# Cross attention scores from upper and lower halves in three products, with both operands split as they are read out of PSUM

## The chip, the cores and the metric

The program runs on one core of a Trainium2 chip. The metric is the device time of one execution in microseconds (us). A difference of 0.2% of this kernel's time is about what a measurement of it can tell from no change.

## The reference, cut to what matters

A block of two layers (feed forward, a mixer, cross attention to a memory of 256 tokens, feed forward) is followed by a second block with another mixer and feed forward. 512 tokens, model width 1024, all in fp32. The change is in the cross attention, which runs once in each of the two layers:

```python
def memory_cross_attention(h, m, w_q, w_kv, q_gain, k_gain, w_o):
    q = rms_norm((h @ w_q).reshape(b, s, X_HEADS, X_HEAD_DIM), q_gain)      # 4 heads of 256
    kv = (m @ w_kv).reshape(b, m.shape[1], 2, X_HEADS, X_HEAD_DIM)
    k = rms_norm(kv[:, :, 0], k_gain)
    v = kv[:, :, 1]
    sc = jnp.einsum('bqhd,bkhd->bhqk', q, k).astype(jnp.float32) * (X_HEAD_DIM ** -0.5)
    p = jax.nn.softmax(sc, axis=-1).astype(v.dtype)
    o = jnp.einsum('bhqk,bkhd->bqhd', p, v).reshape(b, s, X_HEADS * X_HEAD_DIM)
    return o @ w_o
```

## The kernel before, in words

All the large matrix products (`pe_gemm`, `pe_products`) are made from operands split into an upper and a lower half of type fp32r: the weights are brought by DMA into one of four raw buffers, ACT copies them into `wh` (the rounding to fp32r is the upper half), DVE subtracts to get `wl`, and the PE adds three products, upper by upper, upper by lower and lower by upper. Splitting runs three chunks of 256 rows ahead of the PE (`AHEAD`). What belongs to another task (an eviction, a transposition) is put beside certain chunks by the functions called `side` and behind a group by those called `evict`.

One cross attention (class `Cross`, tiles `c0...` in the first layer, `c1...` in the second) runs like this:

- `kv`: four groups of 512 columns, the values first (`c0v`, kept in fp32), then the keys. `xq`: two groups of 512 columns, the queries. For keys and queries ACT copies a 128-token tile into `c0t` and squares it, DVE sums the squares, POOL takes the power, and DVE scales the tile (`dve_head_scale`).
- `pe_turn` transposes such a group, 4 blocks of 128 columns, into four PSUM banks. `act_turned` (L884) reads out the odd blocks and `dve_turned` (L894) the even ones, both times the gain, into `c0kT` (8 blocks of 128x256) and `c0qT` (8 blocks of 128x512), fp32. For keys group 2 this is beside chunk 1 of keys group 3; for keys group 3 beside chunk 1 of queries group 0; for queries group 0 beside chunk 1 of queries group 1; and for queries group 1 it is inside the attention itself, as the function `then`.
- The attention (`pe_whole`, `act_whole`, `dve_whole`, L1295 to L1378) is a pipeline over four heads in steps `s`, below as PE sees it. "Scores" of a head are 8 products (4 tiles of 128 queries, 2 blocks of the head) of 256 columns in fp32; P is the 128x1024 tile of probabilities; "values" are 4 products of 512 columns in fp32.

```
s=0: scores 0
s=1: then (16 transpositions of queries group 1), scores 1, turn P of head 0
s=2: scores 2, turn P of head 1, values 0
s=3: scores 3, turn P of head 2, values 1
s=4: turn P of head 3, values 2        s=5: values 3
```

The order on the other two engines is fixed just so by the code. The lines that decide around the change are these: on both engines `then` comes behind the work of head 0's step 0 and ahead of what follows.

```python
    def act_whole(act, A, finish, then):
        for s in range(A.H + 3):
            if s == 1:
                then()
...
    def dve_whole(dve, A, finish, then):
        for s in range(A.H + 3):
            if s == 1:
                then()
            if 1 <= s <= A.H:
                den, rd = A.small(s - 1, 2), A.small(s - 1, 3)
                dve.wait_ge(expd, (A.tag, s - 1))
```

So ACT does the exponentials of head 0 (`cx0P<-ps,cx0sm`), then its part of the read-out of queries group 1, then the exponentials of head 1. DVE does the maxima of head 0 (`cx0sm<-ps`), then its part of the read-out, then the reciprocal and the scaling of P of head 0 (`cx0P<-cx0P,cx0sm`, L106, four instructions with the flag `normed`), then the maxima of head 1. The PE turns the four rows of a P each when its `normed` is set.

In a profile one fp32 product of the PE appears as two MATMUL records, and each product or record has its own LDWEIGHTS (PEld). Every instruction has the line of its helper: L94 is a matmul, L97 a transpose, L100 an activation, L103 a tensor_tensor, L106 a tensor_scalar, L109 a scalar_tensor_tensor, L118 a reduce, L121 a copy, L124 a reciprocal. In the list of instructions below a buffer's number stands behind its name (`cx0P_149`, `cx0P_150` are the two P tiles), and one fp32 product is one row.

Of the kernel before, what the change touches and what calls it, by code (L numbers as in the profile page):

```python
# [265 lines left out]
def program(nc, T, out):  # L266
# [1004 lines left out]
    class Whole:  # L1271
# [1 line left out]

        groups = [[0, 1], [2, 3]]

        def __init__(self, tag, H, area, scale):
            self.tag, self.H, self.scale = tag, H, scale
            self.p = [sb(f"{tag}P{i}", [P, WHOLE_W], F32, area) for i in range(2)]
            self.pt = [sb(f"{tag}PT{i}", [P, 2, S], F32, area) for i in range(2)]
            self.sm = [sb(f"{tag}sm{i}", [P, 16], F32, area) for i in range(2)]  # L1280
            self.tv = home["xq" + tag[2:], 1]

# [585 lines left out]
    class Cross:  # L1868
        def __init__(self, l):
            st = Area(base)  # L1870
            self.l, self.kv, self.xq = l, f"kv{l}", f"xq{l}"
            self.M = Act(sb(f"c{l}mh", [P, KD, MEM], F32R, st), sb(f"c{l}ml", [P, KD, MEM], F32R, st), MEM, ("M", l))
            self.squares = sb(f"c{l}j", [P, 2, D], F32, st.sub())
            self.tm = [sb(f"c{l}t{i}", [P, NT, 512], F32, st) for i in range(2)]
            self.v = sb(f"c{l}v", [P, 2, D], F32, st)
            self.ss = [sb(f"c{l}ss{i}", [P, NT, 2], F32, st) for i in range(2)]
            self.kT = sb(f"c{l}kT", [P, 8, MEM], F32, st)
            self.qT = sb(f"c{l}qT", [P, 8, S], F32, st)
            self.A = Whole(f"cx{l}", 4, st.sub(), 1.0 / 16)
            self.mgain, self.xgain = par(f"xa_mem_norm{l}"), par(f"xa_norm{l}")  # L1880
            self.qgain, self.kgain = par(f"xa_q_gain{l}"), par(f"xa_k_gain{l}")

# [92 lines left out]
    def xa_bank(C):  # L1975
        return home[C.kv, 1] + 3

    def pe_kv(pe, C):
        def side(g, kp):
            if (g, kp) == (2, 1):  # L1980
                pe_sums(pe, f"xa{C.l}", xa_bank(C), [(total, step, (f"xa{C.l}", "sum", KD - 1))], (1,))
            if (g, kp) == (3, 1):
                pe_turn(pe, C.kv, 2, C.tm[0], 4, 2)
        pe_gemm(pe, C.kv, {"m": C.M}, side)

    def act_kv(act, C):
        def side(g, kp):
            if g < 2 and kp is not None:
                act_upper(act, f"xa{C.l}", f"out{C.l}", 4 * g + kp, last_chunk(f"out{C.l}"))
                act_square(act, f"xa{C.l}", f"out{C.l}", 4 * g + kp)  # L1990
            if (g, kp) == (3, 1):
                act_turned(act, C.kv, 2, 4, 2, lambda c: C.kT[:, c, :], [C.kgain[:, c % 2:c % 2 + 1] for c in range(4)])

        def evict(g):
            if g >= 2:
                act_heads(act, C.kv, g, C.tm[g % 2], 2, 2, 256, 512, None)
                return
            act.wait_ge(summed, (C.kv, g, 1))
            act.wait_ge(turned, (f"mem{C.l}", 3))
            act.activation(C.v[:, 1, 512 * g:512 * (g + 1)], bank[home[C.kv, g] + 1][:, :], AF.Copy).then_inc(  # L2000
                put, (C.kv, "v", g, 1)).also(drained, (C.kv, g, 1))
        act_gemm(act, C.kv, evict, side)

    def dve_kv(dve, C):
        def side(g, kp):
            if g < 2 and kp is not None:
                dve_lower(dve, f"xa{C.l}", 4 * g + kp)
            if (g, kp) == (2, 1):
                dve_means(dve, f"xa{C.l}", xa_bank(C))
            if (g, kp) == (3, 0):  # L2010
                dve_head_scale(dve, C.kv, 2, C.tm[0], C.ss[0], 2, 2, 256)
            if (g, kp) == (3, 1):
                dve_turned(dve, C.kv, 2, 4, 2, lambda c: C.kT[:, c, :], [C.kgain[:, c % 2:c % 2 + 1] for c in range(4)])

        def evict(g):
            if g >= 2:
                dve_head_sums(dve, C.kv, g, C.ss[g % 2], 2, 2, 256)
                return
            dve.wait_ge(summed, (C.kv, g, 0))
            dve.wait_ge(turned, (f"mem{C.l}", 3))  # L2020
            dve.tensor_copy(C.v[:, 0, 512 * g:512 * (g + 1)], bank[home[C.kv, g]][:, :]).then_inc(
                put, (C.kv, "v", g, 0)).also(drained, (C.kv, g, 0))
        dve_gemm(dve, C.kv, evict, side)
# [4 lines left out]
        for g in (2, 3):  # L2028
            pool_head_rates(pool, C.kv, g, C.ss[g % 2], 2, 2, 256)

    def q_dst(C, g):
        return lambda c: C.qT[:, 4 * g + c, :]

    def k_dst(C, g):
        return lambda c: C.kT[:, 4 * g + c, :]

    def by_half(gain):
        return [gain[:, c % 2:c % 2 + 1] for c in range(4)]

    def pe_xq(pe, C):  # L2040
        def side(g, kp):
            if (g, kp) == (0, 1):
# [5 lines left out]
    def act_xq(act, C):  # L2048
        def side(g, kp):
            if (g, kp) == (0, 1):  # L2050
                act_turned(act, C.kv, 3, 4, 2, k_dst(C, 1), by_half(C.kgain))
            if (g, kp) == (1, 1):
                act_turned(act, C.xq, 0, 4, NT, q_dst(C, 0), by_half(C.qgain))
        act_gemm(act, C.xq, lambda g: act_heads(act, C.xq, g, C.tm[g], NT, 2, 256, 512, (C.kv, 2 + g),
                                                        f"xa{C.l}"), side)

    def dve_xq(dve, C):
        def side(g, kp):
            if (g, kp) == (0, 0):
                dve_head_scale(dve, C.kv, 3, C.tm[1], C.ss[1], 2, 2, 256)  # L2060
            if (g, kp) == (0, 1):
                dve_turned(dve, C.kv, 3, 4, 2, k_dst(C, 1), by_half(C.kgain))
            if (g, kp) == (1, 0):
                dve_head_scale(dve, C.xq, 0, C.tm[0], C.ss[0], NT, 2, 256)
            if (g, kp) == (1, 1):
                dve_turned(dve, C.xq, 0, 4, NT, q_dst(C, 0), by_half(C.qgain))
        def evict(g):
            def behind(t):
                if g and t:
                    dve_head_scale(dve, C.xq, 1, C.tm[1], C.ss[1], t, 2, 256, None, t - 1)  # L2070
            dve_head_sums(dve, C.xq, g, C.ss[g], NT, 2, 256, behind)
            if g:
                dve_head_scale(dve, C.xq, 1, C.tm[1], C.ss[1], NT, 2, 256, None, NT - 1)
        dve_gemm(dve, C.xq, evict, side)
# [5 lines left out]
    def pe_cross(pe, C):  # L2080
        A = C.A

        def score(pe, h, i, dst):
            for c in range(2):
                u = 2 * h + c
                pe.wait_ge(put, (C.xq, u // 4, "T", u % 4))
                pe.wait_ge(put, (C.kv, 2 + u // 4, "T", u % 4))
                ins = pe.matmul(dst, C.qT[:, u, i * P:(i + 1) * P], C.kT[:, u, :], start=c == 0, stop=c == 1)
            return ins

        def value(pe, h, PTb):
# [13 lines left out]
    def act_cross(act, C):  # L2105
        def finish(h):
            for c in range(2):
                act.wait_ge(valued, (C.A.tag, h, c))
                act_hi(act, bank[C.A.tv + 2 + c][:, :], hT(f"xo{C.l}"), 2 * h + c, slice(0, S), C.xq)
        act_whole(act, C.A, finish, lambda: act_turned(act, C.xq, 1, 4, NT, q_dst(C, 1), by_half(C.qgain)))  # L2110

    def dve_cross(dve, C):
        def finish(h, c):
            dve.wait_ge(valued, (C.A.tag, h, c))
            dve_lo(dve, bank[C.A.tv + 2 + c][:, :], hT(f"xo{C.l}"), 2 * h + c, slice(0, S)).also(drained, (C.A.tag, "o", h, c))

        dve_whole(dve, C.A, finish, lambda: dve_turned(dve, C.xq, 1, 4, NT, q_dst(C, 1), by_half(C.qgain)))


    sp_area = Area(base)  # L2120
# [847 lines left out]
```

## Time and profile before

| | |
|---|---|
| median of 3 runs | 3131.57 us (3131.51 to 3132.09) |
| the profiled execution | 3131.14 us |
| its span, first to last instruction | 3129.4 us |
| PE busy | 3112.8 us, 99% |
| DVE busy | 1581.1 us, 51% |
| ACT busy | 1220.0 us, 39% |
| POOL busy | 318.2 us, 10% |
| DMA | 290.95 MB, mean 93 GB/s |
| mean granted clock of TensorE | 0.999 |
| the chain that ended last | 97% PE |

A share of busy time says how full an engine was over the whole span; whether an engine waited, and for whom, is in the list of waits and in the timeline. The attention of the first layer lies between 674.57 and 707.74 us of the span, that of the second 1139.63 us later (the first scores behind the transpositions stand at 680.52 and at 1820.15 us in the chain of work that ended last).

### The profile page before, as it was taken

The numbers are of one execution on the slowest core, as the hardware profiler recorded it, in microseconds if no ns is written. First come the engines' busy times: TensorE is split into PE (matmuls) and PEld (weight loads), VectorE is DVE, ScalarE is ACT, GpSimd is POOL, SyncE is SP. The second block draws the span as 40 slices with busy tenths as digits, with TensorE's granted clock in tenths as the row PEclk, the third lists the DMA queues.
The fourth block names the chain that finished last, engine by engine and source line by source line (L and its number), as shares of the span: only waits on it lengthen the run. The fifth ranks groups of instructions, "written<-read, shape, count | busy, mean of one in ns | idle before, by whom it ended". The sixth has DMA issues, their size and how long they took to land.

```text
span 3129.4 us, 37175 instructions
## 1 busy us (share of the span) xinstructions
PE 3112.8 (99%) x14504; PEld 2517.1 (80%) x14504; DVE 1581.1 (51%) x2479; ACT 1220.0 (39%) x2002; POOL 318.2 (10%) x454
## 2 busy tenths in 40 slices
PE   9999999999999999999999999999999999999999
PEld 8888886878888888888867878888887786788887
DVE  5443358754444344433466754443346876564433
ACT  4332247543232233223465543322335727443222
POOL 1000114211000000001210200000142200020000
PEclk9999999999999999999999999999999999999999
DMA  5333321412332233323222413332232231223332
GB/s 159 94 95 101 97 93 35 148 61 88 101 101 95 96 96 93 100 100 96 88 95 81 148 49 100 98 98 94 86 101 81 75 109 33 83 86 95 98 97 74
DMA packets 214368, 290.95 MB, mean 93 GB/s; under 512 B 13072, under 2 KB 138384, under 8 KB 214064
## 3 DMA queue, kind: packets, MB, share of 16 engines
q1 hardware_dynamic: 211120, 279.26, 28.6%
q0 software_dynamic: 2496, 8.98, 0.9%
q8 instruction: 114, 1.87, 0.2%
q14 instruction: 62, 0.51, 0.1%
q10 hardware_dynamic: 576, 0.33, 0.0%
HBM read 286.42 MB, written 2.10 MB: 92 GB/s over the span
## 4 chain that ended last, share of the span: by engine, by line
PE 97%; POOL 1%; DVE 1%; issue 1%; ACT 1%; POOLq 0%; DVEq 0%; ACTq 0%
PE ps L94 94%; PE ps L97 3%; POOL evQ L142 0%; POOL evPb L142 0%; DVE hTl L109 0%; DVE xT L103 0%; DVE s_gb L103 0%; ACT evPb L100 0%; POOL evPa L142 0%; DVE evQ L115 0%; ACT evQ L100 0%; POOL rc L103 0%; ACT evPa L100 0%; ACT xn L100 0%; ACT evPT L100 0%
## 5 line engine op out<-in xcount | busy, mean ns | idle before, releaser
L103 DVE TENSOR_TENSOR wl<-raw,wh 128x1024 fp32r<-128x1024 f32 (+2 forms) x531 | 654.4, 1240 | 1069.6 <-ACT wh L100 1066.9
L100 ACT ACTIVATE wh<-raw 128x1024 fp32r<-128x1024 f32 (+2 forms) x531 | 551.9, 1048 | 1145.7 <-PE ps L94 1105.3
L94 PE MATMUL ps<-hTh,wh 128*128 128x512 f32 x2400 | 942.1, 393 | 0.7 <-ACT hTh L100 0.7
L94 PE MATMUL ps<-hTh,wl 128*128 128x512 f32 x2400 | 937.9, 391 | 0.0
L94 PE MATMUL ps<-hTl,wh 128*128 128x512 f32 x2400 | 895.5, 390 | 0.0
L94 PEld LDWEIGHTS ps<-hTh,wh 128*128 128x128 f32 x2400 | 450.7, 188 | 102.2 <-issue 9.9
L94 PEld LDWEIGHTS ps<-hTh,wl 128*128 128x128 f32 x2400 | 450.7, 188 | 97.2 <-issue 7.1
L94 PEld LDWEIGHTS ps<-hTl,wh 128*128 128x128 f32 x2400 | 449.2, 188 | 96.2 <-issue 4.7
L103 POOL TENSOR_TENSOR xn<-xn 128x512 f32<-128x512 f32 x69 | 98.9, 1433 | 1769.1 <-ACT xn L100 1531.6
L94 PE MATMUL ps<-wh,hTh 128*128 128x512 f32 (+2 forms) x576 | 216.8, 377 | 0.9 <-DVE s_ikT L121 0.9
L94 PE MATMUL ps<-wl,hTh 128*128 128x512 f32 (+2 forms) x576 | 215.1, 374 | 0.0
L94 PE MATMUL ps<-wh,hTl 128*128 128x512 f32 (+2 forms) x576 | 195.1, 374 | 0.0
L94 PEld LDWEIGHTS ps<-wh,hTh 128*128 128x128 f32 x576 | 108.3, 188 | 21.3 <-issue 3.3
L94 PEld LDWEIGHTS ps<-wl,hTh 128*128 128x128 f32 x576 | 108.3, 188 | 19.1 <-issue 1.4
L94 PEld LDWEIGHTS ps<-wh,hTl 128*128 128x128 f32 x576 | 107.1, 188 | 20.2 <-issue 1.8
L109 DVE SCALAR_TENSOR_TENSOR hTl<-xT,prm,hTh 128x512 fp32r<-128x512 f32 x72 | 74.5, 1041 | 15.3 <-ACT hTh L100 14.2
L100 ACT ACTIVATE hTh<-xT,prm 128x512 fp32r<-128x512 f32 x72 | 51.1, 716 | 69.9 <-DVE xT L109 39.8
L94 PE MATMUL ps<-wh,f3Fh 128*128 128x512 f32 x176 | 68.8, 391 | 0.0
L94 PE MATMUL ps<-wl,f3Fh 128*128 128x512 f32 x176 | 68.5, 389 | 0.0
L94 PE MATMUL ps<-f10Fh,wh 128*128 128x512 f32 x176 | 68.5, 389 | 0.0
L94 PE MATMUL ps<-f10Fh,wl 128*128 128x512 f32 x176 | 68.5, 389 | 0.0
L94 PE MATMUL ps<-f20Fh,wh 128*128 128x512 f32 x176 | 68.5, 389 | 0.0
(418 smaller groups left out, 4008.4 us busy)
## 6 DMA issues: line engine op xcount, KB each, us to landing
raw<-in_ffn_w_gu SPq DMA_DIRECT2D x350, 256.0 KB, 3.1
raw<-in_ffn_w_down SPq DMA_DIRECT2D x88, 512.0 KB, 3.5
raw<-in_xa_w_kv SPq DMA_DIRECT2D x32, 512.0 KB, 3.9
raw<-in_w_in SPq DMA_DIRECT2D x28, 512.0 KB, 3.7
raw<-in_od_w_in SPq DMA_DIRECT2D x24, 512.0 KB, 3.6
raw<-in_w_ffn_gate SPq DMA_DIRECT2D x44, 256.0 KB, 2.8
raw<-in_w_ffn_up SPq DMA_DIRECT2D x44, 256.0 KB, 3.1
raw<-in_w_ffn_down SPq DMA_DIRECT2D x22, 512.0 KB, 3.7
```

Of the source, the lines that this page charges most:

```text
L94: return self.made(lambda e: e.matmul(*a, **k))
L97: return self.made(lambda e: e.transpose(*a, **k))
L100: return self.made(lambda e: e.activation(*a, **k))
L103: return self.made(lambda e: e.tensor_tensor(*a, **k))
L109: return self.made(lambda e: e.scalar_tensor_tensor(*a, **k))
```

## The change

- The transposed keys and queries are kept as two tiles each, `c0kTh`, `c0kTl`, `c0qTh`, `c0qTl`, of type fp32r. `act_halves` has ACT read out all four blocks of a group times the gain (upper halves), and `dve_halves` has DVE compute block times gain minus upper half from the same bank with a scalar_tensor_tensor, each behind ACT's flag for that block. The flag for the PE and the bank's release are now DVE's for all four blocks. Before, each engine read out two of four.
- `score` makes three fp32r products of 256 columns in place of one fp32 product.
- The values and the transpositions stay in fp32.
- The P tiles now lie over `c0t`, and the PT tiles over the memory's halves `c0mh`, since the split tiles take more room.

```diff
-        def __init__(self, tag, H, area, scale):
+        def __init__(self, tag, H, area, p_area, pt_area, scale):
             self.tag, self.H, self.scale = tag, H, scale
-            self.p = [sb(f"{tag}P{i}", [P, WHOLE_W], F32, area) for i in range(2)]
-            self.pt = [sb(f"{tag}PT{i}", [P, 2, S], F32, area) for i in range(2)]
+            self.p = [sb(f"{tag}P{i}", [P, WHOLE_W], F32, p_area) for i in range(2)]
+            self.pt = [sb(f"{tag}PT{i}", [P, 2, S], F32, pt_area) for i in range(2)]
...
-            self.kT = sb(f"c{l}kT", [P, 8, MEM], F32, st)
-            self.qT = sb(f"c{l}qT", [P, 8, S], F32, st)
-            self.A = Whole(f"cx{l}", 4, st.sub(), 1.0 / 16)
+            self.kT = [sb(f"c{l}kT{u}", [P, 8, MEM], F32R, st) for u in "hl"]
+            self.qT = [sb(f"c{l}qT{u}", [P, 8, S], F32R, st) for u in "hl"]
+            self.A = Whole(f"cx{l}", 4, st.sub(), p_area, Area(base), 1.0 / 16)
...
+    def act_halves(act, name, g, nt, dst, gain):
+        for c in range(4):
+            act.wait_ge(turned, (name, g, c))
+            act.activation(dst[0][:, 4 * (g % 2) + c, :], bank[home[name, g] + c][:, 0:nt * P], AF.Copy,
+                           scale=gain[:, c % 2:c % 2 + 1]).then_inc(put, (name, g, "hi", c))
+
+    def dve_halves(dve, name, g, nt, dst, gain):
+        for c in range(4):
+            dve.wait_ge(put, (name, g, "hi", c))
+            dve.scalar_tensor_tensor(dst[1][:, 4 * (g % 2) + c, :], bank[home[name, g] + c][:, 0:nt * P],
+                                     gain[:, c % 2:c % 2 + 1], dst[0][:, 4 * (g % 2) + c, :].bitcast(F32), ALU.mult,
+                                     ALU.subtract).then_inc(put, (name, g, "T", c)).also(drained, ("turn", name, g, c))
...
-                ins = pe.matmul(dst, C.qT[:, u, i * P:(i + 1) * P], C.kT[:, u, :], start=c == 0, stop=c == 1)
+                for n, (a, b) in enumerate(((0, 0), (0, 1), (1, 0))):
+                    ins = pe.matmul(dst, C.qT[a][:, u, i * P:(i + 1) * P], C.kT[b][:, u, :], start=c == 0 and n == 0,
+                                    stop=c == 1 and n == 2)
...
-        act_whole(act, C.A, finish, lambda: act_turned(act, C.xq, 1, 4, NT, q_dst(C, 1), by_half(C.qgain)))
+        act_whole(act, C.A, finish, lambda: act_halves(act, C.xq, 1, NT, C.qT, C.qgain))
...
-        dve_whole(dve, C.A, finish, lambda: dve_turned(dve, C.xq, 1, 4, NT, q_dst(C, 1), by_half(C.qgain)))
+        dve_whole(dve, C.A, finish, lambda: dve_halves(dve, C.xq, 1, NT, C.qT, C.qgain))
```

The other three read-outs (both groups of keys, group 0 of the queries) are changed in the same way.

On DVE, at the start of the first layer's attention, before:

```order
L118 TENSOR_REDUCE cx0sm_153<-ps 128x1 x4
L106 TENSOR_SCALAR cx0sm_153<-cx0sm_153 128x4
L106 TENSOR_SCALAR c0qT<-ps,prm 128x512 x2
L124 RECIPROCAL cx0sm_153<-cx0sm_153 128x4
L106 TENSOR_SCALAR cx0P_149<-cx0P_149,cx0sm_153 128x256 x4
```

and with the change (the buffers have other numbers):

```order
L118 TENSOR_REDUCE cx0sm_155<-ps 128x1 x4
L106 TENSOR_SCALAR cx0sm_155<-cx0sm_155 128x4
L109 SCALAR_TENSOR_TENSOR c0qTl<-ps,prm,c0qTh 128x512 x4
L124 RECIPROCAL cx0sm_155<-cx0sm_155 128x4
L106 TENSOR_SCALAR cx0P_151<-cx0P_151,cx0sm_155 128x256 x4
```

Two instructions became four, at the same place: ahead of the reciprocal and the scaling of P of head 0. Each of the four now also reads what ACT writes.

On ACT, at the same place, the piece of the difference:

```order
-L100 ACTIVATE cx0P_149,cx0sm_153<-ps,cx0sm_153 128x256 x4
-L100 ACTIVATE c0qT<-ps,prm 128x512 x2
-L100 ACTIVATE cx0P_150,cx0sm_154<-ps,cx0sm_154 128x256 x4
-L100 ACTIVATE cx0PT_151<-ps 128x2x128 x2
-L100 ACTIVATE cx0P_149,cx0sm_153<-ps,cx0sm_153 128x256 x4
-L100 ACTIVATE cx0PT_152<-ps 128x2x128 x2
+L100 ACTIVATE cx0P_151,cx0sm_155<-ps,cx0sm_155 128x256 x4
+L100 ACTIVATE c0qTh<-ps,prm 128x512 x4
+L100 ACTIVATE cx0P_152,cx0sm_156<-ps,cx0sm_156 128x256 x4
+L100 ACTIVATE cx0PT_153<-ps 128x2x128 x2
+L100 ACTIVATE cx0P_151,cx0sm_155<-ps,cx0sm_155 128x256 x4
+L100 ACTIVATE cx0PT_154<-ps 128x2x128 x2
```

The read-out stays between the exponentials of heads 0 and 1, and has four instructions in place of two.

## Rows read from the trace of the kernel before

**Rows 1.** The profile's page, part 1: busy time, share of span, instructions.

```profile
PE 3112.8 (99%) x14504; PEld 2517.1 (80%) x14504; DVE 1581.1 (51%) x2479; ACT 1220.0 (39%) x2002; POOL 318.2 (10%) x454
```

**Rows 2.** Waits of PE over the span: us in total, times, longest us.

```profile
PE ps L94 <- ACT evQ L100: 5.1, 5, 2.2
...
PE ps L97 <- DVE c1t L103: 0.4, 1, 0.4
PE ps L97 <- DVE c0t L103: 0.4, 1, 0.4
```

**Rows 3.** Timeline, PE, start of layer 0's attention: start us, us, what [idle before].

```profile
674.57 3.61 PE L94 MATMUL ps<-c0kT,c0qT 128*128 128x256 f32 x16
678.02 0.49 PE L97 MATMUL ps<-misc,c0t 128*128 128x128 f32 x3
678.88 1.64 PE L97 MATMUL ps<-misc,c0t 128*128 128x128 f32 x13 [0.37 <-DVE c0t L103]
680.36 3.62 PE L94 MATMUL ps<-c0kT,c0qT 128*128 128x256 f32 x16
683.81 1.04 PE L97 MATMUL ps<-misc,cx0P 128*128 128x128 f32 x8
```

**Rows 4.** Timeline, PE, the rest of it.

```profile
684.69 3.62 PE L94 MATMUL ps<-c0kT,c0qT 128*128 128x256 f32 x16
688.14 1.04 PE L97 MATMUL ps<-misc,cx0P 128*128 128x128 f32 x8
689.02 3.60 PE L94 MATMUL ps<-cx0PT,c0v 128*128 128x512 f32 x8
692.45 3.62 PE L94 MATMUL ps<-c0kT,c0qT 128*128 128x256 f32 x16
695.90 1.04 PE L97 MATMUL ps<-misc,cx0P 128*128 128x128 f32 x8
...
700.21 1.04 PE L97 MATMUL ps<-misc,cx0P 128*128 128x128 f32 x8
701.09 7.22 PE L94 MATMUL ps<-cx0PT,c0v 128*128 128x512 f32 x16
707.74 0.79 PE L94 MATMUL ps<-hTh,wh 128*128 128x512 f32 x1
```

**Rows 5.** Timeline, PE, 256-column fp32r products of an earlier stage (`in0`).

```profile
395.74 0.28 PE L94 MATMUL ps<-wl,hTh 128*128 128x256 f32 x1
...
400.42 0.28 PE L94 MATMUL ps<-wl,hTh 128*128 128x256 f32 x1
```

**Rows 6.** Timeline, DVE, layer 0's attention, heads 0, 1 and 3.

```profile
678.13 0.69 DVE L103 TENSOR_TENSOR c0t<-c0t,c0ss 128x512 f32<-128x512 f32 x1 [0.59 <-POOL c0ss L103]
...
682.58 1.14 DVE L106 TENSOR_SCALAR cx0P<-cx0P,cx0sm 128x256 f32<-128x256 f32 x4
...
687.46 1.14 DVE L106 TENSOR_SCALAR cx0P<-cx0P,cx0sm 128x256 f32<-128x256 f32 x4
...
699.28 1.14 DVE L106 TENSOR_SCALAR cx0P<-cx0P,cx0sm 128x256 f32<-128x256 f32 x4
```

**Rows 7.** Timeline, ACT, around the read-out of queries group 1.

```profile
680.40 0.47 ACT L100 ACTIVATE cx0P<-ps,cx0sm 128x256 f32<-128x256 f32 x1 [3.06 <-DVE cx0sm L106]
...
682.21 1.28 ACT L100 ACTIVATE c0qT<-ps,prm 128x512 f32<-128x512 f32 x2
```

**Rows 8.** Groups by shape, DVE: busy us, mean ns of one | idle before.

```profile
L109 DVE SCALAR_TENSOR_TENSOR hTl<-xT,prm,hTh 128x512 fp32r<-128x512 f32 x72 | 74.5, 1041 | 15.3 <-ACT hTh L100 14.2
...
L109 DVE SCALAR_TENSOR_TENSOR hTl<-ps,prm,hTh 128x512 fp32r<-128x512 f32 x8 | 5.6, 744 | 1.7 <-ACT hTh L100 1.7
```

**Rows 9.** Timeline, the last scalar_tensor_tensors of the program.

```profile
3125.55 0.75 DVE L109 SCALAR_TENSOR_TENSOR x_back<-xn,stat,x_back 128x512 f32<-128x512 f32 x1
3126.22 0.75 DVE L109 SCALAR_TENSOR_TENSOR x_back<-f3sg,stat,x_back 128x512 f32<-128x512 f32 x1
```

**Rows 10.** Timeline, ACT, after the read-outs of keys group 2 and queries group 0.

```profile
622.66 0.91 ACT L100 ACTIVATE c0kT<-ps,prm 128x256 f32<-128x256 f32 x2 [2.04 <-PE ps L97]
...
625.83 0.60 ACT L100 ACTIVATE c0t<-ps 128x512 f32<-128x512 f32 x1 [1.31 <-PE ps L94]
...
666.61 0.69 ACT L100 ACTIVATE c0t<-ps,rc 128x512 f32<-128x512 f32 x1 [1.10 <-PE ps L94]
```

**Rows 11.** Timeline, PE: the longest wait, and the last product.

```profile
499.51 1.14 PE L94 MATMUL ps<-e_kbT,e_qbT 64*128 64x384 f32 x8 [2.17 <-ACT evQ L100]
...
3123.58 0.39 PE L94 MATMUL ps<-wh,f3Fl 128*128 128x512 f32 x1
```

**Rows 12.** Busy time by stretch; PEclk is the granted clock, behind POOL.

```profile
499.00:501.00 2.00, 1.49 (x13) 1.20 (x13) 0.15 (x1) 2.00 (x5) 0.56 (x3) 1.00 0.00 0
...
3126.00:3126.50 0.50, 0.00 (x0) 0.00 (x0) 0.50 (x2) 0.00 (x0) 0.00 (x0) 0.50 0.00 0
```

More of the change, by code:

```diff
@@ L1873, in __init__ @@
             self.squares = sb(f"c{l}j", [P, 2, D], F32, st.sub())
+            p_area = st.sub()
             self.tm = [sb(f"c{l}t{i}", [P, NT, 512], F32, st) for i in range(2)]
@@ L1991, in side @@
             if (g, kp) == (3, 1):
-                act_turned(act, C.kv, 2, 4, 2, lambda c: C.kT[:, c, :], [C.kgain[:, c % 2:c % 2 + 1] for c in range(4)])
+                act_halves(act, C.kv, 2, 2, C.kT, C.kgain)
         def evict(g):
@@ L2012, in side @@
             if (g, kp) == (3, 1):
-                dve_turned(dve, C.kv, 2, 4, 2, lambda c: C.kT[:, c, :], [C.kgain[:, c % 2:c % 2 + 1] for c in range(4)])
+                dve_halves(dve, C.kv, 2, 2, C.kT, C.kgain)
         def evict(g):
@@ L2029, in pool_kv @@
             pool_head_rates(pool, C.kv, g, C.ss[g % 2], 2, 2, 256)
[L2031 to L2038, printed above, removed]
     def pe_xq(pe, C):
@@ L2050, in side @@
             if (g, kp) == (0, 1):
-                act_turned(act, C.kv, 3, 4, 2, k_dst(C, 1), by_half(C.kgain))
+                act_halves(act, C.kv, 3, 2, C.kT, C.kgain)
             if (g, kp) == (1, 1):
-                act_turned(act, C.xq, 0, 4, NT, q_dst(C, 0), by_half(C.qgain))
+                act_halves(act, C.xq, 0, NT, C.qT, C.qgain)
         act_gemm(act, C.xq, lambda g: act_heads(act, C.xq, g, C.tm[g], NT, 2, 256, 512, (C.kv, 2 + g),
@@ L2061, in side @@
             if (g, kp) == (0, 1):
-                dve_turned(dve, C.kv, 3, 4, 2, k_dst(C, 1), by_half(C.kgain))
+                dve_halves(dve, C.kv, 3, 2, C.kT, C.kgain)
             if (g, kp) == (1, 0):
@@ L2065, in side @@
             if (g, kp) == (1, 1):
-                dve_turned(dve, C.xq, 0, 4, NT, q_dst(C, 0), by_half(C.qgain))
+                dve_halves(dve, C.xq, 0, NT, C.qT, C.qgain)
         def evict(g):
```

## The prediction

> **What bounds the kernel now.** I read the page first: the PE is busy for 99% of the span [rows 1]. Then the PE's list of waits: in 3129.4 us it waits a few times only, and in both cross attentions the one wait listed is 0.4 us for the scaling of the last query tile [rows 2]. So the kernel is bound by the PE's own work, also here, and whatever shortens that shortens the time, as long as the other engines keep up. Whether they do is read in the timeline of one attention, engine by engine. The second layer has the same waits [rows 2] and I take it as equal; each term below counts twice.
>
> The PE's timeline [rows 3, 4] has no hole but that wait: scores 0 from 674.57, the transpositions of queries group 1 with the wait in them, scores 1 from 680.36, turn P of head 0 from 683.81, scores 2, turn, values 0, scores 3, turn, values 1, turn from 700.21, values 2 and 3 from 701.09, next stage at 707.74. What the reader should see is how thin the cover is. DVE scales P of head 0 from 682.58 to 683.72 [rows 6], and the PE begins to turn it at 683.81 [rows 3]. For head 1 it is 687.46 to 688.60 [rows 6] against 688.14 to 689.02 [rows 4]: again just in time. The softmax chain of DVE and ACT is nearly as long as the PE's work in the first steps.
>
> **The change, part by part.**
>
> *Scores.* A head's 8 fp32 products take 683.81 - 680.36 = 3.45 us of the PE, 0.431 each [rows 3]. The new form, three fp32r products of 256 columns with a 128x128 stationary, stands in an earlier stage: 40 starts from 395.74 to 400.42, 4.68 / 39 = 0.120 us each [rows 5]. A head becomes 24 x 0.120 = 2.88 us: 0.57 less, and 8 x 0.57 = 4.6 us less over both layers, if all of it counts. The nearest other price is the record of the fp32 product, 3.45 / 16 = 0.216 us, with which a head would cost 5.2; I leave it out, since rows 5 are the very same form and length. The Trainium skill, page "TensorE: Matmul & The Clock Gate", section "Back-to-back issue gap", gives a product alone N / 2.4 ns plus some 2.5 ns, an estimate of 0.109 us for 256 columns; the row says 0.120. By the page a head would be another 0.26 us shorter, and the sum below 0.5 us smaller, since only head 3's share gets through. The row stands, as it has a new stationary load for each product as here.
>
> *Scores 0.* Their 0.57 us is worth nothing: the transpositions behind them need the last query tile, which DVE has only at 678.13 + 0.69 = 678.82 [rows 6], and PE's wait until 678.88 becomes 0.57 us longer. Scores 1 still start at 680.36, and end at 683.24.
>
> *Read-out of queries group 1, inside the attention.* This is the costly part. The maxima of head 0 stand behind that same scaling on DVE, so ACT's exponentials still start at 680.40 and its read-out at 682.21 [rows 7]. ACT now reads out four blocks: 682.21 + 0.69 = 682.90 for the first, then one each 0.60 (two took 1.28). Before, DVE did its two blocks while ACT was still at the exponentials. Now it can begin only at 682.95, behind ACT's first block, and has four scalar_tensor_tensors. From PSUM with an fp32r result one takes 744 ns [rows 8], and two in a row start 0.67 us apart [rows 9]. The last ends at 682.95 + 3 x 0.67 + 0.74 = 685.70. The reciprocal overlaps it a little (as instructions on DVE do) and the scaling of P of head 0 starts at about 685.84 in place of 682.58 [rows 6]: **3.26 us later**. Bounds: with the dearer row, 1041 ns, whose source is in SBUF [rows 8], four cost 1.2 us more; below, they cannot come faster than ACT's 0.60, 0.2 us less. I take 744, the row with our source.
>
> *What the delay does to the PE.* It is at P of head 0 at 683.24, and the last row is ready at 685.84 + 1.14 = 686.98; two transpositions later, at 687.3, it starts scores 2, against 684.69 [rows 4]: +2.6. The PE stands still from 683.24 to about 686.2. Behind P of head 0 on DVE wait the maxima of head 1, behind them ACT's exponentials of head 1, and behind those P of head 1: all 3.26 later, so P of head 1 is scaled from 690.72 to 691.86. Scores 2 end at 687.3 + 2.88 = 690.2, the PE waits again for about 0.9, and values 0 start at about 692.15 against 689.02: +3.13. Now values 0 (3.43 us) give the chain air: scores 3 run from 695.58 to 698.46, P of head 2 was ready at 696.75. That is +2.56 against 695.90, for head 3's 0.57 are earned. P of head 3 before was scaled from 699.28, 3.38 behind the end of scores 3 [rows 4, 6]; now 701.84 to 702.98, while the PE is at it from 702.77: no wait. Values 2 and 3 and the next stage are +2.56.
>
> *The other three read-outs* (keys twice, queries group 0) take ACT two instructions more, 0.8 us for the keys and 1.2 for the queries, and DVE about as much plus the lag behind ACT. ACT's next deadline behind them still has it idle for 1.31 and 1.10 us, for the PE [rows 10]: it just fits, and weights are split three chunks ahead. I cost them at nothing; if that cover is gone, it is some tenths of a us each. The moved P and PT tiles lie over tiles whose last readers ended before: nothing.
>
> **Sum.** 2 x 2.56 = 5.1 us. Against the profiled execution, 3131.14, that gives 3136.3; the median of the runs is 0.43 higher, so the forecast is 3131.57 + 5.1 = **3136.7 us**, 0.16% more. What a measurement can tell is 0.2%, 6.3 us: the likeliest result is on the near side of it, but not by much.
>
> **The rivals.**
>
> *A. The PE's clock falls in the stall* (slower, 0.23). The longest wait of the PE so far is 2.17 us, and the granted clock was 1.00, 2.4 GHz, in the stretch behind it [rows 11, 12]. At the end of the program the last product ends at 3123.97 and the clock is at 0.50, 1.2 GHz, from 3126.0 [rows 11, 12], after 2.0 us of rest. The new stall is 2.9 us, longer than either. If the clock falls, the transpositions and scores 2 behind it run at half speed. If it is back after half of scores 2, these end 1.4 later, 0.9 of it covered by the wait for P of head 1, and the turn is longer: about +0.75. If only after the turn, 2.88 + 0.87 - 0.9 plus what the delay of the maxima adds, about +2.8. So it gives 3131.57 + 5.1 + 0.75 (one layer, short) up to + 5.6 (both, long): 3137.4 to 3142.3, with 3139 in the middle. It is over the 0.2% from 1.2 us of such loss. That speaks for it: the end of the program. Against it: the 2.17 us wait, and that between the two heads' stalls the PE does work. On the Trainium skill, same page, section "Why this matters for your kernels": it warns that idle gaps between bursts of matmuls bring the clock back to half; the trace agrees at the end of the span, and not at the 2.17 us wait.
>
> *B. The scalar_tensor_tensors cost what the SBUF row says* (slower, 0.08). +1.2 us a layer: 3139.1. Against it: eight instructions of exactly this form at 744 ns.
>
> *C. The stall does not come* (0.08). It needs P of head 0 scaled by 683.2, which means the new work fits into DVE's and ACT's pauses. Even so scores 0 earn nothing and P of head 0 (683.72 today) and of head 1 (688.60) hold the PE, so heads 1 and 2 earn 0.1 together, and head 3 its 0.57: -0.7 a layer, 3130.2. The 4.6 us of the plain count would give 3127.0. Both are within 0.2%, hence there is hardly a way to be faster by more.
>
> *D. The read-outs in the projections make the weights late* (0.05). They are the ones with the least slack beside them (1.1 us). With 0.5 us at each of the six places: +3, 3139.7.
>
> **How the numbers follow.** My forecast 0.56, A 0.23, B 0.08, C 0.08, D 0.05. Slower by over 0.2%: most of A (0.18), B and D (0.11), and a tail of the forecast (0.04): 0.33. Faster by over 0.2%: 0.02. Within: 0.65. The range leaves out C and the long form of A: 3133.5 to 3140.5.
>
> **What would show it.** In the profile after: scores of a head in 2.88 us on the PE; scores 1 starting 5.8 us behind scores 0 as before; ACT's read-out of four at the end of head 0's exponentials, DVE's four from 0.7 us behind it; the scaling of P of head 0 beginning 5.4 us behind ACT's first exponential (2.2 before); two waits of the PE in each layer, about 2.9 and 0.9 us, on DVE's `cx0P`; and the next stage 35.7 us behind scores 0 (33.17 before). The granted clock there decides A. The forecast is wrong if the wait for P of head 0 is under 2 us, if the waits appear at head 2 or 3, or if the PE waits for weights in the projections.

## The result, and the profile after

| | before | with the change |
|---|---|---|
| median of 12 runs, us | 3131.79 | 3137.75 |
| lowest to highest, us | 3131.49 to 3132.65 | 3137.07 to 3139.06 |
| ratio, 95% interval | | 1.0019 [1.0012, 1.0027] |
| profiled execution, us | 3131.14 | 3138.19 |
| its span, us | 3129.4 | 3136.5 |

The change costs 6.0 us, 0.19%: the interval does not hold 1.0, and the time is within the range that was forecast. It is just under the 0.2% that the chances of the prediction were set by. Two single runs of what follows lie far above all others, 6371.75 us (of the version with two blocks ahead and two behind) and 3707.97 us (of the kernel before, beside it); the ratios leave them out, and nothing on record explains them beyond a mean granted clock of 0.79 in the second.

The busy times on the profile's page hardly tell of it:

```profile
PE 3112.4 (99%) x14568; PEld 2520.3 (80%) x14568; DVE 1589.4 (51%) x2495; ACT 1226.8 (39%) x2018; POOL 316.1 (10%) x454
```

Against [rows 1] the PE has 64 more records (32 a layer: 96 products of one record each, where there were 32 of two) and is busy for 0.4 us less. DVE has 8.3 us more, ACT 6.8 us, and both still have half of the span idle, or nearly. Nothing here looks like a kernel that has become slower. The waits of the PE do (total, times, longest, us):

```profile
PE ps L94 <- ACT evQ L100: 4.9, 5, 2.2
PE ps L97 <- DVE cx1P L106: 2.9, 1, 2.9
PE ps L97 <- DVE cx0P L106: 2.9, 1, 2.9
...
PE ps L97 <- DVE c0t L103: 1.0, 1, 1.0
PE ps L97 <- DVE c1t L103: 1.0, 1, 1.0
...
PE ps L97 <- DMA misc<-in_misc: 0.6, 1, 0.6
```

New against [rows 2] is one wait of 2.9 us in each layer for P of a head, and the wait for the last query tile has grown from 0.4 to 1.0 us. The second wait for P that was forecast, about 0.9 us at head 1, is not there. The PE's timeline of layer 0's attention tells why (start, length, what, idle before it; the products of a scores step have one row each now, so the first and last of a step stand here):

```profile
675.90 0.28 PE L94 MATMUL ps<-c0kTh,c0qTh 128*128 128x256 f32 x1
...
678.66 0.28 PE L94 MATMUL ps<-c0kTh,c0qTl 128*128 128x256 f32 x1
678.78 0.49 PE L97 MATMUL ps<-misc,c0t 128*128 128x128 f32 x3
680.22 1.64 PE L97 MATMUL ps<-misc,c0t 128*128 128x128 f32 x13 [0.95 <-DVE c0t L103]
681.62 0.36 PE L94 MATMUL ps<-c0kTh,c0qTh 128*128 128x256 f32 x1
...
687.62 1.94 PE L97 MATMUL ps<-misc,cx0P 128*128 128x128 f32 x8 [2.89 <-DVE cx0P L106]
689.21 0.56 PE L94 MATMUL ps<-c0kTh,c0qTh 128*128 128x256 f32 x1
...
692.93 1.03 PE L97 MATMUL ps<-misc,cx0P 128*128 128x128 f32 x8
693.80 3.60 PE L94 MATMUL ps<-cx0PT,c0v 128*128 128x512 f32 x8
...
711.93 0.80 PE L94 MATMUL ps<-hTh,wh 128*128 128x512 f32 x1
```

Scores 0 take 678.78 - 675.90 = 2.88 us, 24 products 0.12 apart. The transpositions of P of head 0 (687.62) need 1.59 us to scores 2 in place of 0.88 [rows 3, 4], and scores 2 need 692.93 - 689.21 = 3.72 us in place of 2.88. The busy time by stretch names the reason (stretch, its length, busy PE, PEld, DVE, ACT, POOL, then the granted clock); the last two stretches are of layer 1:

```profile
687.50:690.50 3.00, 2.88 (x14) 2.91 (x15) 2.92 (x10) 0.67 (x3) 0.00 (x0) 0.50 0.00 0
690.50:691.50 1.00, 1.00 (x9) 1.00 (x9) 0.00 (x0) 1.00 (x5) 0.00 (x0) 0.80 0.00 0
1831.00:1834.00 3.00, 3.00 (x16) 3.00 (x15) 1.89 (x7) 1.70 (x7) 0.00 (x0) 0.50 0.03 5
1834.50:1836.00 1.50, 1.50 (x16) 1.50 (x15) 1.50 (x6) 0.28 (x2) 0.00 (x0) 1.00 0.00 0
```

The PE's clock is at 0.50, 1.2 GHz, for 3.4 us in each layer, behind the new stall, and at 2.4 GHz before and after.

The chain behind the stall, on DVE:

```profile
680.08 1.41 DVE L118 TENSOR_REDUCE cx0sm<-ps 128x1 f32<-128x256 f32 x4
...
684.28 2.73 DVE L109 SCALAR_TENSOR_TENSOR c0qTl<-ps,prm,c0qTh 128x512 fp32r<-128x512 f32 x4 [2.58 <-ACT c0qTh L100]
686.92 0.17 DVE L124 RECIPROCAL cx0sm<-cx0sm 128x4 f32<-128x4 f32 x1
687.12 1.14 DVE L106 TENSOR_SCALAR cx0P<-cx0P,cx0sm 128x256 f32<-128x256 f32 x4
...
692.01 1.14 DVE L106 TENSOR_SCALAR cx0P<-cx0P,cx0sm 128x256 f32<-128x256 f32 x4
```

and on ACT:

```profile
681.74 0.47 ACT L100 ACTIVATE cx0P<-ps,cx0sm 128x256 f32<-128x256 f32 x1 [3.06 <-DVE cx0sm L106]
...
683.55 2.43 ACT L100 ACTIVATE c0qTh<-ps,prm 128x512 fp32r<-128x512 f32 x4
```

DVE stands idle for 2.58 us because its first scalar_tensor_tensor needs ACT's first block, begins 0.73 us behind ACT's start, runs four in a row, and only then comes to the reciprocal and P of head 0: 687.12 - 681.74 = 5.38 us behind ACT's first exponential, where it was 2.18 [rows 6, 7].

**Where the 7.1 us between the two spans are.** From scores 0 to the next stage an attention took 33.17 us; it now takes 711.93 - 675.90 = 36.03 us, and 36.08 in layer 1 (33.18 before). That is 2.86 + 2.90 = 5.76 us. Between the first attention and the second both traces have the same 1106.45 us (all the profiled executions of this document have it, within 0.06). The other 1.33 us lie ahead of the first attention, which starts at 675.90 in place of 674.57. Of these, 0.46 are there by the PE's longest wait, which ends at 499.97 in place of 499.51 [rows 11], in code that is the same in all the kernels. The other 0.87 come behind that wait, and they are the clock again. It fell to 0.50 there too, in this execution and not in that of before:

```profile
499.97 2.08 PE L94 MATMUL ps<-e_kbT,e_qbT 64*128 64x384 f32 x8 [2.16 <-ACT evQ L100]
```

```profile
500.50:503.00 2.50, 2.50 (x13) 1.76 (x10) 1.69 (x2) 1.66 (x5) 0.01 (x1) 0.50 0.03 7
```

That this is not the change's doing is seen in the run of the products alone, below: it splits nothing, the clock fell there as well, and its first attention starts at 676.04. So it is no surprise that the medians differ by less, 5.96 us, than the two profiled executions, 7.05.

### The profile page after: what moved, and what is told of

The parts are those of the page before. It is cut to its first block, busy times and chain, and to the rows that moved or that the text cites. A ratio compares the mean times of both kernels' runs of the same rounds, so it can differ in the third digit from the quotient of the medians.

```text
span 3136.5 us, 37333 instructions
## 1 busy us (share of the span) xinstructions
PE 3112.4 (99%) x14568; PEld 2520.3 (80%) x14568; DVE 1589.4 (51%) x2495; ACT 1226.8 (39%) x2018; POOL 316.1 (10%) x454
## 4 chain that ended last, share of the span: by engine, by line
PE 94%; issue 3%; DVE 1%; POOL 1%; ACT 0%; DMA 0%; ACTq 0%; POOLq 0%; DVEq 0%
PE ps L94 91%; PE ps L97 3%; POOL evQ L142 0%; POOL evPb L142 0%; DVE hTl L109 0%; DVE xT L103 0%; DMA prm<-in_prm 0%; DVE s_gb L103 0%; POOL evPa L142 0%; DVE evQ L115 0%; DVE c1qTl L109 0%; DVE c0qTl L109 0%; POOL rc L103 0%; ACT cx0P L100 0%; ACT cx1P L100 0%
## 5 line engine op out<-in xcount | busy, mean ns | idle before, releaser
L94 PE MATMUL ps<-f21Fh,wl 128*128 128x512 f32 x176 | 68.5, 389 | 0.0
L94 PE MATMUL ps<-f20Fh,wl 128*128 128x512 f32 x176 | 68.5, 389 | 0.0
```

Of the source, the lines that this page charges most:

```text
L94: return self.made(lambda e: e.matmul(*a, **k))
```

## The experiments

The question was not only whether the sum came out, but whether it did so for its reasons: the read-out of queries group 1 as the whole of the loss, nothing earned from most of the cheaper products, nothing lost in the projections, and then the clock. Lengths are of an attention from scores 0 to the next stage, layer 0 and layer 1, in the profiled execution of each kernel.

**The read-outs without the products.** Against the change:

```diff
-                for n, (a, b) in enumerate(((0, 0), (0, 1), (1, 0))):
-                    ins = pe.matmul(dst, C.qT[a][:, u, i * P:(i + 1) * P], C.kT[b][:, u, :], start=c == 0 and n == 0,
-                                    stop=c == 1 and n == 2)
+                ins = pe.matmul(dst, C.qT[0][:, u, i * P:(i + 1) * P].bitcast(F32), C.kT[0][:, u, :].bitcast(F32),
+                                start=c == 0, stop=c == 1)
```

> The read-outs of the change (four blocks on ACT, four on DVE behind it), but each score as one fp32 product as before, made from the upper halves; the lower halves are written and not used. Chain theory (the read-out of queries group 1 delays the scaling of P of head 0 by 3.3 us): P of head 0 and of head 1 come as late as in the changed kernel, and head 3's 0.57 us are not earned, so +3.1 us a layer, 3138.1 us, with waits of the PE of about 2.3 and 0.4 us for cx0P; some tenths more if the clock falls. Rival, the products are what costs: 3131.8, as before the change.

Measured: 3139.35 us (3137.46 to 3140.65, 10 runs), ratio 1.0022 [1.0013, 1.0032]. Both attentions took 36.29 us, 3.1 more than before. The PE's timeline, at P of head 0:

```profile
680.42 3.62 PE L94 MATMUL ps<-c0kTh,c0qTh 128*128 128x256 f32 x16
686.35 1.14 PE L97 MATMUL ps<-misc,cx0P 128*128 128x128 f32 x8 [2.31 <-DVE cx0P L106]
```

With the old products the stall is shorter by what they take longer, 2.31 against 2.89 us, and a second wait of 0.29 us stands at P of head 1: the loss is the read-out's. The clock stayed at 1.00 in both attentions of this execution. By length alone the median should be near 3138; it is 1.3 us above that, and the profiled execution was the fastest of the ten. That the clock fell in the attentions of others of them would explain it; only the one has a trace.

**The products without the read-outs.** The three products all take the upper halves, which ACT and DVE read out two and two as before; the lower halves are not made.

```diff
-                for n, (a, b) in enumerate(((0, 0), (0, 1), (1, 0))):
+                for n, (a, b) in enumerate(((0, 0), (0, 0), (0, 0))):
...
-        act_whole(act, C.A, finish, lambda: act_halves(act, C.xq, 1, NT, C.qT, C.qgain))
+        act_whole(act, C.A, finish, lambda: act_plain(act, C.xq, 1, NT, C.qT, C.qgain))
...
-        dve_whole(dve, C.A, finish, lambda: dve_halves(dve, C.xq, 1, NT, C.qT, C.qgain))
+        dve_whole(dve, C.A, finish, lambda: dve_plain(dve, C.xq, 1, NT, C.qT, C.qgain))
```

(`act_plain` and `dve_plain` are `act_turned` and `dve_turned` into the upper half; the other three read-outs are changed alike. The scores of this kernel lack their lower halves.)

> Three fp32r products per score as in the change, all three from the upper halves; the read-outs as before, two blocks on ACT and two on DVE, and the lower halves are left out. Chain theory: no wait for cx0P over 0.3 us, scores of head 3 earn 0.57 and the others 0.1 a layer: 3130.4 us, clock at 1.00 throughout. Rival, all 4.6 us of the plain count are earned: 3127.2. Rival, the products are what costs: about 3137.7.

Measured: 3130.8 us (3130.2 to 3132.34), ratio 0.9997 [0.9987, 1.0006]; length 32.51 in both layers, 0.66 less than before. So of the 2.3 us a layer that the products save, the PE's own work, 0.66 reaches the end. The rest turned into waits, at the last query tile and at P of head 1:

```profile
PE ps L97 <- DVE c0t L103: 1.0, 1, 1.0
...
PE ps L97 <- DVE cx0P L106: 0.8, 1, 0.8
```

The expectation had the time right and the place of a wait wrong (it had none over 0.3 us for P). P of head 0 shows no wait, although the PE comes to it 0.57 us earlier. The plain count's 3127.2 is refuted: the softmax chain alone, with no new work on it, takes back seven tenths of the gain.

**Only queries group 1 read out as before.** The other three read-outs keep both halves; heads 2 and 3 take the upper half of the queries twice. The lines of `act_plain` and `dve_plain` for group 1 are as in the run before this one; the one of the products is:

```diff
-                for n, (a, b) in enumerate(((0, 0), (0, 1), (1, 0))):
+                for n, (a, b) in enumerate(((0, 0), (0, 1), (h < 2, 0))):
```

> The changed kernel, but queries group 1 (the one read out inside the attention) is read out as before, upper halves only, two blocks on each engine; heads 2 and 3 use the upper half in place of the lower one of the queries. Keys and queries group 0 are split as in the change. Chain theory: the read-outs in the projections cost nothing, so as with the products alone, 3130.4 us. Rival, the read-outs in the projections make something late: 3132 or more, with waits of the PE for wl or hTl between 590 and 675 us.

Measured: 3130.41 us (3130.2 to 3131.04), ratio 0.9994 [0.9985, 1.0003]; length 32.51, as in the run before this one. The read-outs in the projections cost nothing that can be measured, and rival D falls. All of the difference from this kernel to the change, 7.3 us by the medians, is the read-out inside the attention and what it sets off.

**The change, with the PE kept busy in the stall.** Ten products of `ones` (`pe_warm`), twenty records in the profile, go into the bank that the transpositions of P of head 0 write next:

```diff
                     pe.held[b] = (A.tag, s - 1, "t", n)
+                    if s == 1 and not n:
+                        pe_warm(pe, b, 10)
```

> The changed kernel, with 10 products of ones (128x128, about 0.26 us each) into the bank of the first turn, ahead of the turn of P of head 0: the PE works in the stall. Clock theory as one part of the loss (layer 0 and 1 each lose about 0.3 us to a clock at 0.50 for 3.4 us): granted clock 1.00 in the attention, next stage 2.56 us later than before in place of 2.9, 3137.1 us. Rival, the clock is the main cause: 3134 or less. Rival, the clock costs nothing since the waits cover it: 3137.7.

Measured: 3137.12 us (3136.72 to 3137.66, 11 runs), ratio 1.0015 [1.0006, 1.0024]; length 35.72 and 35.71. The timeline:

```profile
684.29 2.50 PE L94 MATMUL ps<-ones 128*128 128x128 f32 x20 [0.35 <-DVE c0qTl L109]
686.74 1.23 PE L97 MATMUL ps<-misc,cx0P 128*128 128x128 f32 x8
687.73 0.36 PE L94 MATMUL ps<-c0kTh,c0qTh 128*128 128x256 f32 x1
...
690.55 0.28 PE L94 MATMUL ps<-c0kTh,c0qTl 128*128 128x256 f32 x1
691.72 1.14 PE L97 MATMUL ps<-misc,cx0P 128*128 128x128 f32 x8 [0.89 <-DVE cx0P L106]
692.69 3.60 PE L94 MATMUL ps<-cx0PT,c0v 128*128 128x512 f32 x8
...
710.83 0.79 PE L94 MATMUL ps<-hTh,wh 128*128 128x512 f32 x1
```

The clock is 1.00 up to the last product. The 0.35 us ahead of the fillers are a wait for their bank: it holds block 0 of queries group 1 until DVE's first scalar_tensor_tensor has read it. This is the forecast without rival A, and it has both of its waits: the one at P of head 0, filled, and 0.89 us at P of head 1. Its length is what the sum gave (35.73). The low clock of the change costs 0.3 us in layer 0 and 0.4 in layer 1 beyond that, since the transpositions and scores 2 at half speed used up the wait of 0.89 us. The runs also lie closer together, within 0.9 us where the change's lie within 2.0.

These four ran beside the same runs of before (median 3131.87 us). Of those that follow, P of head 0 first, ACT first and two and two ran beside a median of 3132.18 us, and the other three beside one of 3132.01 us.

**P of head 0 scaled ahead of the split.** On DVE alone the order is changed:

```diff
     def dve_whole(dve, A, finish, then):
         for s in range(A.H + 3):
-            if s == 1:
-                then()
             if 1 <= s <= A.H:
...
+            if s == 1:
+                then()
```

> The changed kernel with one order on DVE: the reciprocal and the scaling of P of head 0 ahead of the four scalar_tensor_tensors of queries group 1. Chain theory: the stall moves and is not gone. P of head 0 is in time (no wait of the PE over 0.2 us there), scores 2 wait about 0.4 us for the split queries, the maxima of head 1 start 2.7 us later than before the change, so the PE waits some 3 us for P of head 1; values 0 about 2.5 us late, next stage +1.9 a layer: 3135.7 us. Rival, only P of head 0 matters: about 3130.5.

Measured: 3138.03 us (3136.2 to 3140.28), ratio 1.0019 [1.0009, 1.0028]; length 36.86 and 36.85. Missed by 2.3 us. The stall is not gone, as expected, but it came in two pieces, and behind the second the clock fell, now under values 0. The PE's timeline, and its stretches below:

```profile
684.82 1.31 PE L97 MATMUL ps<-misc,cx0P 128*128 128x128 f32 x8 [1.04 <-DVE c0qTl L109]
...
690.99 1.19 PE L97 MATMUL ps<-misc,cx0P 128*128 128x128 f32 x8 [1.98 <-DVE cx0P L106]
...
691.97 5.29 PE L94 MATMUL ps<-cx0PT,c0v 128*128 128x512 f32 x8
```

```profile
692.00:695.00 3.00, 3.00 (x6) 1.31 (x5) 1.78 (x6) 1.81 (x8) 0.00 (x0) 0.50 0.00 0
695.50:697.00 1.50, 1.50 (x6) 0.64 (x4) 1.01 (x4) 0.67 (x2) 0.00 (x0) 1.00 0.00 0
```

The first wait is not for P of head 0. DVE's timeline has it scaled in time:

```profile
682.96 1.15 DVE L106 TENSOR_SCALAR cx0P<-cx0P,cx0sm 128x256 f32<-128x256 f32 x4
684.02 2.73 DVE L109 SCALAR_TENSOR_TENSOR c0qTl<-ps,prm,c0qTh 128x512 fp32r<-128x512 f32 x4
```

All four rows are ready at 684.11, and the PE turns the first at 684.82. What it lacked is the bank. The transpositions of P use two banks that hold blocks 0 and 1 of queries group 1 before, and with the change a bank is free only behind DVE's scalar_tensor_tensor of its block. The first of these ends at about 684.02 + 0.74 = 684.76. In the change itself the same wait is hidden in the longer one for P.

**The same, with the PE kept busy.** To tell the order's own worth from the clock's, the version above gets filler products ahead of P of head 1:

```diff
             if 1 <= s <= A.H:
+                if s == 2:
+                    pe.wait_ge(drained, pe.held[A.tv + 2])
+                    pe_warm(pe, A.tv + 2, 8)
```

> The kernel with the scaling of P of head 0 first on DVE (the run where the clock fell to 0.50 from 691.9 to 695.3 us, during values 0), with 8 products of ones on the PE in its wait for P of head 1. Theory: that low clock cost half of 3.4 us, 1.7 a layer, since nothing covers values 0; without it an attention takes 36.86 - 1.7 = 35.15 us from scores 0 to the next stage, and the time is about 3135.9 us with a small spread. Rival, the low clock was covered there too: 36.8 us and 3138 as before.

Measured: 3135.88 us (3135.53 to 3136.65), ratio 1.0012 [1.0003, 1.0021]; length 35.12 in both layers, clock 1.00. As expected. It is also the length that was expected of the version above, 1.95 us a layer over before against 1.9: what that expectation lacked was the clock. The order earns 0.6 us a layer against the change with the PE kept busy (35.72), and the low clock had cost the version above 36.86 - 35.12 = 1.74 us a layer.

**ACT's read-out ahead of the exponentials.** ACT waits for the scores' maxima for 3.06 us [rows 7]; its four blocks are put in front, with a one-column exponential ahead of them. In ACT's timeline the load of the exponentials' table (`ACT_TABLE_LOAD`, 1.28 us) stands in front of it and not between the blocks and head 0.

```diff
     def act_whole(act, A, finish, then):
+        act.activation(A.small(0, 2)[:, 0:1], ones[:, 0:1], AF.Exp).then_inc(step, (A.tag, "table"))
+        act.wait_ge(step, (A.tag, "table"))
         for s in range(A.H + 3):
-            if s == 1:
+            if s == 0:
                 then()
```

> The changed kernel with one order on ACT: the four upper halves of queries group 1 ahead of the exponentials of head 0, so that DVE can split them while ACT does the exponentials (the exp table is loaded by a one-column activation before). Chain theory: exponentials of head 0 start 0.8 to 1.0 us later, DVE's four end by 683.2 on the layer's clock of before, P of head 0 in time, P of head 1 0.4 us late, head 3 earns 0.57: -0.2 a layer against before, 3131.5 us, clock 1.00. Rival, DVE's four instructions themselves are what delays (not their wait for ACT): about 3135.

Measured: 3133.21 us (3132.88 to 3133.83), ratio 1.0003 [0.9994, 1.0012]; length 33.75, 0.58 more than before where 0.2 less was expected. The timeline of ACT:

```profile
680.10 2.43 ACT L100 ACTIVATE c0qTh<-ps,prm 128x512 fp32r<-128x512 f32 x4 [1.76 <-PE ps L97]
682.40 0.49 ACT L100 ACTIVATE cx0P<-ps,cx0sm 128x256 f32<-128x256 f32 x1
```

I had counted ACT's idle time as room, but the blocks are there to be read out only after 1.76 us of it, so the exponentials were pushed back by more than a microsecond. It does settle what stalls the change: DVE still has its four scalar_tensor_tensors and does them in its own idle time, and 2.3 of the 2.9 us are gone. So it is the place of the work in the chain that costs, not the work. Waits of 0.91 and 0.89 us remain at P of heads 0 and 1.

**Two blocks ahead, two behind.** ACT reads out blocks 0 and 1 before the exponentials of head 0 and 2 and 3 after them; DVE splits 0 and 1 before it scales P of head 0, and 2 and 3 after the maxima of head 1.

```diff
+        act.activation(A.small(0, 2)[:, 0:1], ones[:, 0:1], AF.Exp).then_inc(step, (A.tag, "table"))
+        act.wait_ge(step, (A.tag, "table"))
...
-            if s == 1:
-                then()
+            if s < 2:
+                then(2 * s)
...
             if s == 1:
-                then()
+                then(0)
...
+                if s == 1:
+                    then(2)
```

> The changed kernel with blocks 0 and 1 of queries group 1 read out by ACT ahead of the exponentials of head 0 and blocks 2 and 3 behind them; DVE splits blocks 0 and 1 ahead of the scaling of P of head 0, and 2 and 3 behind the maxima of head 1 (only head 3 needs them). Chain theory: P of head 0 and head 1 as before the change, head 3 earns its 0.57: -0.5 a layer, 3130.8 us, clock 1.00. Rival as for the run before: about 3134.

Measured: 3131.2 us (ratio 0.9995 [0.9986, 1.0004]); length 32.60 in both layers, 32.67 expected, clock 1.00. All of the change's loss is gone and the products' 0.6 a layer is earned, as far as the trace goes; by the times it is even with before.

**The chain of head 0 ahead of everything.** The shortest order I found for the changed kernel, by 0.06 us in the traces: DVE takes the maxima of head 0 before it scales the last query tile (the PE turns the queries tile by tile, so that it has the other three meanwhile), then P of head 0, two blocks, the maxima of head 1, two blocks.

```diff
-            if s == 1:
-                then()
...
+            if s == 1:
+                then(0)
...
+                if s == 0:
+                    last()
+                if s == 1:
+                    then(2)
...
-            if g:
-                dve_head_scale(dve, C.xq, 1, C.tm[1], C.ss[1], NT, 2, 256, None, NT - 1)
...
-        pe_whole(pe, A, score, value, lambda: pe_turn(pe, C.xq, 1, C.tm[1], 4, NT))
+        pe_whole(pe, A, score, value, lambda: pe_turn_rows(pe, C.xq, 1, C.tm[1], 4, NT))
```

> The changed kernel with another order around the start of the attention: DVE does the maxima of head 0 ahead of the scaling of the last query tile, then the scaling of P of head 0, the split of blocks 0 and 1, the maxima of head 1 and the split of blocks 2 and 3; the PE turns queries group 1 tile by tile, the last tile last; ACT as in the change. Chain theory: the exponentials of head 0 start 1.2 us earlier, P of head 1 some 0.4 us earlier than before the change: 32.2 us an attention (33.17 before, 36.05 with the change), 3130.0 us, clock 1.00. Rival, the chain is not what ends last: 32.6 or more.

Measured: 3130.55 us (3130.16 to 3131.27), ratio 0.9996 [0.9987, 1.0005]; length 32.54 and 32.53, 32.2 expected. It is 7.2 us under the change. The 1.5 us under before are not shown: the interval holds no change. DVE's timeline shows where the rest of the wait went:

```profile
681.48 1.14 DVE L106 TENSOR_SCALAR cx0P<-cx0P,cx0sm 128x256 f32<-128x256 f32 x4
682.54 1.41 DVE L109 SCALAR_TENSOR_TENSOR c0qTl<-ps,prm,c0qTh 128x512 fp32r<-128x512 f32 x2
683.86 1.41 DVE L118 TENSOR_REDUCE cx0sm<-ps 128x1 f32<-128x256 f32 x4
...
687.68 1.14 DVE L106 TENSOR_SCALAR cx0P<-cx0P,cx0sm 128x256 f32<-128x256 f32 x4
```

P of head 0 is ready before the PE wants it; P of head 1, behind two splits, the maxima and two more splits, is not, and the PE waits 0.65 us for it. The last query tile, scaled behind the maxima, costs it another 0.81 us.

**The kernel before in the same order.** The same moves, without the halves:

```diff
-            if s == 1:
-                then()
...
+            if s == 1:
+                then()
...
+                if s == 0:
+                    last()
```

> The kernel before (fp32 scores, read-out two and two, no halves) with the same reorder on DVE and PE. Theory: the PE's own work ends last throughout, the wait for the last query tile is gone: 32.8 us an attention, 3131.0 us. Then the three products earn about 0.6 us a layer once the chain is out of the way. Rival, the reorder does it all: 32.2 us.

Measured: 3132.14 us (3131.71 to 3132.79), ratio 1.0000 [0.9992, 1.0009]; length 33.22 and 33.21, no shorter than 33.17. Missed: the last query tile is now scaled after the maxima, so the PE still waits 0.3 us for it, where I had it waiting for nothing. In nearly the same order the three products earn 33.22 - 32.54 = 0.68 us a layer, which agrees with the 0.66 of the products alone.

## Why the prediction held

**Scores, 2.88 us a head: right.** The change's products are 0.120 us apart, as [rows 5] had them.

**Scores 0 earn nothing: right.** The wait for the last query tile is 0.95 us, as worked out.

**The read-out delays P of head 0: right.** 5.38 us behind the first exponential against 5.44 forecast, DVE's start 0.73 behind ACT's (0.74). The four instructions have a mean of 745 ns by the profile's groups, so [rows 8] was read at the right form, and rival B falls.

**The stall, +2.56 a layer at the end: right, but for the clock.** With the PE kept busy the attention is 35.72 us long, the sum gave 35.73, and the 0.9 us wait at head 1 is there. No wait appears at heads 2 and 3. Rival C, no stall, falls with it.

**The projections cost nothing: right**, by the run that keeps three of the four read-outs.

**Mis-sized: rival A.** The forecast itself held the clock at 1.00 in the stall. In the profiled execution it fell in both layers. So the rival that I gave 0.23 is what happened there, and the forecast's mechanism is right without being all of it. Its price was wrong too: 0.75 us a layer in the short form, against 0.3 and 0.4 measured (36.03 and 36.08 against 35.72 and 35.71). P of head 1 is scaled 692.01 - 687.12 = 4.89 us behind P of head 0, as in [rows 6] (4.88), so the low clock did not move the chain. Counted from scores 0 of layer 0, the next turn starts at 17.03 us (692.93 - 675.90) where it starts at 16.61 (691.72 - 675.11) with the PE kept busy: 0.42 later, the rest went into the wait. And that turn is 0.10 us shorter, 0.87 against 0.97, since all its rows are ready, where the sum had it longer. With the low clock a layer costs 2.88, two cost 5.8, and the medians say 5.96. The two medians are known to some tenths at best, so the 0.2 us between are nothing to explain. Without the clock it would be 5.1, and the run with the PE kept busy says 3137.12 - 3131.87 = 5.25.

The Trainium skill, page "TensorE: Matmul & The Clock Gate", section "Why this matters for your kernels", warns that long idle gaps between bursts of matmuls bring the clock back to half speed. These runs agree at the 2.89 us waits of the change. Its warning is of long gaps only, so the wait of 2.17 us behind which the clock stayed up [rows 11, 12] did not speak against it, as the prediction had it.

**Two readings of the prediction that did not hold.** Against rival A it set the 2.17 us wait. That was one execution: in the change's own the clock fell behind the same wait, and so it did in seven of the twelve profiled executions of this document. The row was no evidence against the rival. And it took the end of the scaling of P of head 0 (683.72) as what holds the PE; but the PE turns each row as it comes, and the products alone left no wait there, only 0.8 us at P of head 1. That changes nothing in the sum, as heads 1 and 2 together still earn the 0.1 us it had.

**What it did not have: the banks.** With the change the transpositions of P of head 0 also wait for DVE to release their bank. Here P comes later still, so the sum does not feel it; with P scaled first it is a wait of 1.04 us.

**What stays open.** How often the clock falls in the runs that have no trace. For those only the mean granted clock of the whole span is known: 0.998 or 0.999 in the change's twelve, 0.999 or 1.000 in the eleven with the PE kept busy. Within the change's twelve, the five of 0.999 took 3137.07 to 3137.52 us and the seven of 0.998 took 3137.49 to 3139.06, so the longer runs are those of the lower clock. That fits the wider spread, but doesn't count the falls or say where they were. The 1.3 us of the read-outs alone rest on the same guess.

## What to carry to other kernels

An engine that is busy for half of the span can still set the time: count what it does between one result that the bound engine waits for and the next, here DVE between the exponentials and P, where the slack was some 0.1 us and four instructions in place of two put P 3.2 us later. Before work is added on such a chain, ask for its place first: the same instructions, put where DVE and ACT wait anyway, cost nothing (32.5 us against 36.0). Ask also who frees the buffers that the bound engine writes next. And a cheaper product on the bound engine is worth only what the chain beside it lets through: here 0.7 of 2.3 us a layer.

## What the runs showed of the hardware

- The clock fell in the change behind one rest of 2.89 us, and in the version with P scaled first behind rests of 1.04 and 1.98 us with 4.2 us of work between them; it stayed up behind 2.31 us in the read-outs alone. So the length of the last rest alone does not decide.
- The same program at the same place can go either way. All twelve profiled executions have the wait of 2.16 to 2.20 us near 500 us of the span, in code that no version changed. The clock fell behind it in seven (the change, the read-outs alone, the products alone, both with P of head 0 first, ACT first, two and two) and stayed up in five, that of before among them [rows 11, 12]. From there to the first attention it took 175.02 to 175.06 us where the clock stayed up and 175.37 to 175.93 where it fell. So one profiled execution does not tell whether a clock will fall, and differences of some tenths of a us between two executions may be this.
- It did not always fall before the PE resumed: in layer 0 of the change it is at 0.50 from 687.5 us, as the PE resumes at 687.62; in layer 1 from about 1831.0, 0.9 us after it resumed:

```profile
1830.09 1.27 PE L97 MATMUL ps<-misc,cx1P 128*128 128x128 f32 x8 [2.89 <-DVE cx1P L106]
```

- Each low stretch in the attentions lasted 3.41 us, in the change and with P scaled first, in both layers. The same 3.41 us cost 0.3 to 0.4 us where the PE had a wait ahead of it to use up, and 1.74 us where values 0 followed, on which all else hangs.
- At 1.2 GHz the 256-column products start 0.213 us apart, where it is 0.120 at 2.4 GHz: not quite twice.
